# HGRN outputs moved among the value products, HGRN states among the raw products, and the compression done batch by batch

## The reference, cut to what matters

```python
# HGRN2, per head: outputs from products inside a chunk and from the state, and the new state
o     = einsum(A, v) + einsum(q * exp(b), S)
S_new = exp(b_last) * S + einsum(k * exp(b_last - b), v)
o_h   = rms_norm(o, hgrn_norm) * silu(gate)
# NSA compression: 32 raw rows (16 new ones per step) to one key and one value
hid = sum(einsum(chunks[r : r + n] + pe[r], w1[r]) for r in range(2))
out = einsum(silu(hid), w2)                 # kc = rms_norm(out for keys), vc = out for values
```

## Time and profile before

| | us |
|---|---|
| median of 3 runs | 1907.07 (1905.36 to 1914.19) |
| the profiled execution: its time | 1915.5 |
| its span, first to last instruction | 1913.5 |
| TensorE busy | 1779.4 (93%) |
| VectorE busy | 1060.0 (55%) |
| ScalarE busy | 545.4 (29%) |
| GpSimd busy | 143.2 (7%) |
| mean granted TensorE clock | 0.952 of 2.4 GHz |

### The profile page before, as it was taken

The page is one execution under the profiler, slowest core; times in us unless marked ns, Lnnn a source line. Parts: engine busy times, 40 slices in busy tenths (PEclk is TensorE's granted clock), DMA queues, the critical chain, the costliest instruction groups (busy, mean ns, idle before and its releaser), DMA issues.

```text
span 1913.5 us, 28184 instructions
## 1 busy us (share of the span) xinstructions
PE 1779.4 (93%) x11320; PEld 1518.9 (79%) x11320; DVE 1060.0 (55%) x1513; ACT 545.4 (29%) x781; POOL 143.2 (7%) x135
## 2 busy tenths in 40 slices
PE   6999999999769898999999999999999876999998
PEld 6999976776548574468999987999987544999996
DVE  6776623536531664425776636776623734777642
ACT  5443210102101361313343224333211221433321
POOL 1000020000001121101000011110010000000010
PEclk9999998999869898989999999999999788999999
DMA  4445454212234400624677424677433624343432
GB/s 176 153 153 194 143 168 140 82 49 88 103 120 133 149 1 30 216 90 185 234 262 262 154 88 175 237 264 271 151 135 110 261 103 162 130 142 145 175 111 72
DMA packets 50798, 287.80 MB, mean 150 GB/s; under 512 B 8004, under 2 KB 21344, under 8 KB 26624
## 3 DMA queue, kind: packets, MB, share of 16 engines
q1 hardware_dynamic: 41840, 233.90, 33.9%
q0 software_dynamic: 4272, 46.53, 6.7%
q10 hardware_dynamic: 4608, 6.29, 1.0%
HBM read 280.51 MB, written 41.62 MB: 168 GB/s over the span
## 4 chain that ended last, share of the span: by engine, by line
PE 82%; DVE 9%; ACT 3%; DMA 3%; issue 2%; SPq 1%; POOLq 0%; POOL 0%; DVEq 0%; ACTq 0%
PE ps L687 15%; PE ps L689 15%; PE ps L688 15%; PE ps L699 6%; PE ps L1338 6%; PE ps L1387 4%; PE ps L2155 2%; DVE w_lo L678 2%; PE ps L1568 2%; ACT w_hi L672 2%; PE ps L1271 2%; DVE mem L666 1%; PE ps L1696 1%; PE ps L1543 1%; PE ps L885 1%
## 5 line engine op out<-in xcount | busy, mean ns | idle before, releaser
L687 PE MATMUL ps<-x_hi,w_hi 128*128 128x320 f32 x1408 | 439.1, 312 | 29.1 <-DVE w_lo L678 22.3
L688 PE MATMUL ps<-x_lo,w_hi 128*128 128x320 f32 x1408 | 437.4, 311 | 0.0
L689 PE MATMUL ps<-x_hi,w_lo 128*128 128x320 f32 x1408 | 437.2, 311 | 0.0
L678 DVE TENSOR_TENSOR w_lo<-live,w_hi 128x2048 fp32r<-128x2048 f32 (+1 forms) x120 | 300.7, 2506 | 180.7 <-ACT w_hi L672 180.7
L672 ACT ACTIVATE w_hi<-mem 128x2048 fp32r<-128x2048 f32 (+1 forms) x120 | 250.3, 2086 | 259.1 <-DVE mem L666 259.1
L687 PEld LDWEIGHTS ps<-x_hi,w_hi 128*128 128x128 f32 x1408 | 266.2, 189 | 34.4 <-DVE w_lo L678 25.5
L688 PEld LDWEIGHTS ps<-x_lo,w_hi 128*128 128x128 f32 x1408 | 266.4, 189 | 0.0
L689 PEld LDWEIGHTS ps<-x_hi,w_lo 128*128 128x128 f32 x1408 | 266.3, 189 | 0.0
L687 PE MATMUL ps<-act_hi,w_hi 128*128 128x320 f32 x704 | 219.0, 311 | 6.3 <-DVE w_lo L678 6.3
L689 PE MATMUL ps<-act_hi,w_lo 128*128 128x320 f32 x704 | 218.3, 310 | 0.0
L688 PE MATMUL ps<-act_lo,w_hi 128*128 128x320 f32 x704 | 218.2, 310 | 0.0
(11 more groups left out here) (388 smaller groups left out, 2021.8 us busy)
## 6 DMA issues: line engine op xcount, KB each, us to landing
live<-in_w_fi SPq DMA_DIRECT2D x88, 1024.0 KB, 4.8
live<-in_w_fo SPq DMA_DIRECT2D x32, 1408.0 KB, 6.1
mem<-in_dil SPq DMA_DIRECT2D x16, 1152.0 KB, 11.0
out_old_dil<-in_old_dil POOLq DMA_DIRECT2D x8, 2032.0 KB, 9.1
live<-in_w_even SPq DMA_DIRECT2D x12, 1024.0 KB, 4.8
mem<-in_slc SPq DMA_DIRECT2D x48, 192.0 KB, 2.7
live<-in_w_gate SPq DMA_DIRECT2D x8, 1024.0 KB, 4.8
out_old_dil<-in_old_dil POOLq DMA_DIRECT2D x8, 1008.0 KB, 7.5
```

Of the source, the lines that this page charges most:

```text
L678: nc.vector.tensor_tensor(w_lo[:, slot, 0:w], ring[:, slot, 0:w], w_hi[:, slot, 0:w].bitcast(F32), ALU.subtract).then_inc(w_split.sem, 1)
L687: nc.tensor.matmul(out, wh, hi, start=first_k, stop=False)
L688: nc.tensor.matmul(out, wh, lo, start=False, stop=False)
L689: return nc.tensor.matmul(out, wl, hi, start=False, stop=last_k)
```

## The change

Ten parts, as the diff has them.

- **Outputs among value products.** `pe_hgrn_output(c)` is called inside `pe_values`: pairs 0 and 1 after the second and third token tile of chunk 2, pairs 2 and 3 after the second and third of chunk 3. They use banks 6 and 7 in turn, so pair c (2, 3) waits for `hn_done` 9 + c, the multiply of pair c − 2.
- **Their norms are norms 10 to 13** of the same sequence, with banks 4 and 5 and the same tiles and semaphores. Statistics 10 and 11 follow the first and second tile of chunk 3, 12 and 13 the transposes.
- **VectorE.** `dve_hgrn_gate(0)` stands after norm 9, ahead of the last chunk's evacuation; gate 1 after it; then the copies of the transposed keys, gates 2 and 3, and the states.
- **ScalarE.** Page issues of batch 0 (`act_raw(0)`) stand between the root of norm 11 and the square of norm 13.
- **States.** Transposes go to banks 0 to 3, the prompt's states to bank 6, and sample states 2 to 7 stand after each of the six groups of raw batch 0. Raw batch 1 waits for the last of them added.
- **Constants.** `w1c`, `w2c`, `pe_in` lie over the HGRN queries and forget gates, the others over tiles that are dead when the decays are done; SyncE loads them ahead of the stores, on `hg_kd`.
- **Pages.** Batch 1 into `raw[1]` waits for the fourth output only.
- **Prompt's rows first.** They are the 16 extra columns of batch 0, and ScalarE copies them.
- **Per batch.** SiLU, keys, values, squares, root, reciprocal and multiply are done for each batch; on TensorE the keys and values of batch j − 1 follow the fourth group of batch j, its squares the sixth. Those of batch 3 stand in the prompt attention, which begins at the sums of batch 3. Of the fillers, 5 + 6 go and 3 come.
- **Sample attention** waits for all four batches' keys (SyncE's cache loads and TensorE's compressed scores).

```diff
-            pe.wait_ge(hrt_ready.sem, 10)
-            pe.wait_ge(evac.sem, first["even_o", 0])
-            pe_hgrn_outputs(pe)
+            pe_hgrn_turned(pe)
+            pe_head_norm(pe, "even", range(12, 14))
             pe_compress(pe)
...
                     pe_head_norm(pe, which, norms[tt:tt + 1])
+                    if which == "even":
+                        if (j, tt) == (2, 1):
+                            pe_hgrn_output(pe, 0)
+                        elif (j, tt) == (2, 2):
+                            pe_hgrn_output(pe, 1)
+                        elif (j, tt) == (3, 0):
+                            pe_head_norm(pe, which, range(10, 11))
+                        elif (j, tt) == (3, 1):
+                            pe_head_norm(pe, which, range(11, 12))
+                            pe_hgrn_output(pe, 2)
+                        elif (j, tt) == (3, 2):
+                            pe_hgrn_output(pe, 3)
...
+            square(0)
+            for n in range(14):
+                if n == 12:
+                    act_raw(act, 0)
+                if n + 1 < 14:
+                    square(n + 1)
+                act.wait_ge(hms_ready.sem, n + 1)
+                if n >= 2:
+                    act.wait_ge(hn_done.sem, n - 1)
+                nc.scalar.activation(rt2[:, n % 2, :], ps[:, 4 + n % 2, 0:TOK], ACT.Sqrt, bias=eps[:])\
+                    .then_inc(hrt_ready.sem, 1)
...
                     stream("even_v", 0)
+                    sp_compress(sp)
                     sp_save_even(sp)
-                    sp_compress(sp)
...
         def sp_compress(sp):
+            sp.wait_ge(hg_kd.sem, 1)
...
             elif j == 1:
-                cm_loaded.wait(pool, NCM)
+                pool.wait_ge(hg_o.sem, 4)
...
+            pe_hgrn_prompt_states(pe)
+            for hh in range(2):
+                pe_hgrn_sample_state(pe, hh)
             for j in range(NB // 2):
...
-                if j >= 2:
+                if j == 0:
+                    pe.wait_ge(cm_in.sem, 1)
+                elif j == 1:
+                    pe.wait_ge(hg_stc.sem, 5)
+                else:
                     pe.wait_ge(cm_sum.sem, j - 1)
...
+                    if g == 5:
+                        last.then_inc(cm_out.sem, 1)
+                    if j == 0:
+                        pe_hgrn_sample_state(pe, 2 + g)
+                    elif g == 3:
+                        pe_compress_keys_values(pe, j - 1)
+                    elif g == 5:
+                        pe_compress_squares(pe, j - 1)
...
+            for j in range(NB // 2):                    # ScalarE
+                if j + 2 < NB // 2:
+                    act_raw(act, j + 2)
+                act.wait_ge(cm_sum.sem, j + 1)
...
+            for j in range(NB // 2):                    # VectorE
+                dve_compress_sums(dve, j, chain)
+                if j + 1 < NB // 2:
+                    dve_compress_values(dve, j, chain)
+                    dve_compress_keys(dve, j, chain)
...
         def pe_prompt(pe):
-            cm_done.wait(pe)
+            pe.wait_ge(cm_done.sem, 1)
+            pe.wait_ge(cm_sum.sem, NB // 2)
...
             scores(0)
             scores(1)
+            pe_compress_keys_values(pe, NB // 2 - 1)
...
             pe_unread(7, 2)
+            pe_compress_squares(pe, NB // 2 - 1)
...
+                elif t == 0:
+                    pe_unread(7, 3)
+                    pe.wait_ge(cm_vc.sem, NB // 2)
+                    pe.wait_ge(cm_rt.sem, NB // 2)
...
+                if t == 2:
+                    dve_compress_keys(dve, NB // 2 - 1, chain)
```

More of the change, by code:

```diff
@@ L353, in build @@
         pst = sb([P, 3, 12])
+        assert place[0] <= shared + T_Q * TOK
         place[0] = shared + WIN + L_W
@@ new lines, in pe_hgrn_output @@
+        def pe_hgrn_output(pe, c):
+            if c == 0:
+                hg_kd.wait(pe)
+                pe.wait_ge(evac.sem, first["even_v", 0] + 2)
+            if c >= 2:
+                pe.wait_ge(hn_done.sem, 9 + c)
+            for g in range(2):
+                r, hh = slice(64 * g, 64 * g + 64), 2 * c + g
+                v = slice(C_HI + HD * hh, C_HI + HD * hh + HD)
+                o = ps[r, 6 + c % 2, :]
+                nc.tensor.matmul(o[:, 0:TP], vtok[:, 0, v], at[:, hh, 0:TP], start=True, stop=False,
+                                 skip_group_check=True)
+                nc.tensor.matmul(o[:, P:TP], vtok[:, 1, v], at[:, hh, TP:TP + P], start=False, stop=False,
+                                 skip_group_check=True)
+                nc.tensor.matmul(o[:, TP:TOK], vtok[0:64, 2, v], at[0:64, hh, 384:448], start=False, stop=False,
+                                 skip_group_check=True)
+                for b in range(NB):
+                    last = nc.tensor.matmul(o[:, TP + TS * b:TP + TS * b + TS], s0[:, c, b, :],
+                                            qe[:, g, c, TS * b:TS * b + TS], start=False, stop=(b == NB - 1),
+                                            skip_group_check=True)
+            last.then_inc(hg_o.sem, 1)
@@ L1595, in act_compress, with pe_compress_squares @@
-        def act_compress(act):
+        def pe_compress_squares(pe, j):
+            pe.wait_ge(cm_sq.sem, j + 1)
+            if j:
+                pe.wait_ge(cm_rt.sem, j)
+            w = NC_COLS if j == 0 else P
+            nc.tensor.matmul(ps[:, 6, 0:2 * w], ones_h[:], ksq[:, :, 0:w], start=True, stop=True).then_inc(cm_ms.sem, 1)
+        def act_compress(act):
+            for j in range(6):
+                for s2 in range(2):
+                    r = 64 * (j % 2)
+                    src = proj[r:r + 64, T_CMP + j // 2, 0:TP].rearrange("p (m c s t) -> p m s c t", m=2, s=8, t=2)
+                    dst = raw[0][64 * s2:64 * s2 + 64, 2 * PAGES:, 64 * j:64 * j + 64]
+                    last = nc.scalar.activation(dst.rearrange("p m (s c) -> p m s c", s=8), src[:, :, :, :, s2], ACT.Copy)
+            last.then_inc(cm_in.sem, 1)
+            act_raw(act, 1)
@@ new lines, in dve_compress_sums @@
+        def dve_compress_sums(dve, j, chain):
+            n = NC_COLS if j == 0 else 2 * PAST // 16
+            v = ps[:, 2 * (j % 2):2 * (j % 2) + 2, 0:3 * NC_COLS].rearrange("p a (g n) -> p a g n", g=3)
+            dve.wait_ge(cm_out.sem, j + 1)
+            if j:
+                dve.wait_ge(cm_sum.sem, j)
+            chain(nc.vector.tensor_copy(hsum[:, :, :, 0:n - 1], v[64:P, :, :, 1:n]))
+            chain.settle()
+            parts = [(0, NCMP_S, P * j), (64, NCMP_S, P * j + 64)] + [(P, NCMP_P, 512)] * (j == 0)
+            for k, (c, m, to) in enumerate(parts):
+                last = nc.vector.tensor_tensor(hid[:, :, :, to:to + m], v[0:64, :, :, c:c + m], hsum[:, :, :, c:c + m], ALU.add)
+                if k + 1 < len(parts):
+                    chain(last)
+            last.then_inc(cm_sum.sem, 1)
```

308 lines of the change are left out of this document (144 added, 164 removed).

## The result

| | before | changed |
|---|---|---|
| median, us | 1914.37 (20 runs, 1904.49 to 1937.53) | 1904.71 (20 runs, 1890.44 to 1919.07) |
| ratio to before | | 0.9947, 95% interval 0.9927 to 0.9966 |
| profiled execution: time, span | 1915.5, 1913.5 | 1896.5, 1894.5 |
| mean granted clock | 0.952 | 0.959 |

The page's first row for the changed kernel, busy time of each engine, says as little as the mean clock does: TensorE 94% where it was 93%.

A forecast was written before the change was run, and what follows sets the result against it. TensorE, busy 93% of the span, was taken as the bound, leaving gaps and low clock to win: 25.5 + 9.9 − 6.5 − 1 = 27.9 us, from 1907.07 to 1879 us; range 1868 to 1889, with rivals 1 and 2 1865 to 1895.

The forecast's parts named there:

- Up to the first raw product: Stage ending at the first raw product: start at 534 and not 559.5, a gain of 25.5 us.
- 9.9 us: Gain forecast from first raw product to first prompt scores: 69.2 us instead of 79.1.
- ScalarE's page issue for batch 2 ... lies ahead of that SiLU and ends at 557.5, hidden: Before batch 0's SiLU: 7.65 us of page issue costs nothing; TensorE waits 1.5 us before batch 0's keys.
- six sample states of 0.54 each: In raw batch 0: state products added to 12.9 us of raw products, making 16.1 us.
- The wait before keys 1: TensorE's wait for SiLU before the keys and values of batch 1, forecast at 2.9 us.
- 6.5 us lost: From first scores to first transposes: batch 3's keys, squares and fillers at low clock, 14.9 us against 8.4 before.
- 1 us lost: Prompt attention loop: 2 us of VectorE work on batch 3's keys costs 1 us (0 to 2).
- Rival 1: Before raw batch 0: POOL's page issues wait for VectorE, 8 us later, 1887 us; chance 5%.
- Rival 2: Raw batches: serial per-batch chains make waits some 7 us each, 16 us more lost, 1895 us; chance 12%.
- Rival 3: Low clock persists through raw batches, perhaps into the prompt loop: 40 us slower than before, 1947 us; chance 4%.
- Rival 4: Outputs only change place, gaps reappear whole behind gates 2 and 3, nothing won: 1907 us; chance 3%.
- my own signs: Wrong if first transposes come under 18 us earlier, clock low in raw batches 1–3, or later stages change over 2 us.

The follow-up runs named there:

- e5: Changed kernel, ScalarE issuing batch 2's pages before waiting for the position bias, and hidden rows over dead tiles, not waiting for the sample states' store; 1898.29 us, ratio 0.9901.
- e12: Changed kernel with the edits of e5 and e9, odd pages issued by SyncE, sample state products in pairs, fillers before outputs 2 and 3, first keys, scores; 1868.85 us, 0.9772.
- e8: Changed kernel plus products nobody reads before the keys of batches 0 and 1 (8 and 3) and before the first scores (5); 1889.77 us, ratio 0.9871.
- e9: Changed kernel, but VectorE computes batch 3's keys ahead of turn 0 of the prompt attention instead of in turn 2; 1892.36 us, ratio 0.9889.
- e6: Changed kernel, all batches' keys, values, squares, roots, reciprocals after the last raw product, pages of batches 2 and 3 issued together ahead of the SiLUs; 1894.96 us, 0.9895.
- e1: Changed kernel, but ScalarE issues the pages of batch 2 before it waits for the position bias; 1901.16 us, ratio 0.9941.
- e2: Changed kernel, hidden rows over dead tiles so their sums skip waiting for the sample states' store, prompt's state stored early; 1906.65 us, ratio 0.9969.
- e11: e6 plus the edit of e9 and fillers before outputs 2 and 3 (2 and 4) and the first scores (5); 1881.20 us, ratio 0.9827.

## Why the prediction was wrong, step by step

*Up to the first raw product: right in its waits, in part by luck in its sum.* From output 0 on, 58.7 us forecast, 58.2 measured; waits of 1.5 and 4.2 forecast, 1.52 and 4.00 measured. The place of the clock was off. It had fallen by 498, behind the 1.52 us wait already, came back near 504 and fell again behind the second wait; output 2 was slower than I had it, and the constants were faster, 3.7 us for the 7.0 of the earlier trace rows. A wait of 1.82 us for VectorE's spread values, which I had ready by then, was missing. That these cancel to 0.5 us is luck.

*"9.9 us" from there to the first scores: wrong, it was a loss of 4.3* (83.6 us against 79.3 before and 69.2 forecast). The terms:
- "ScalarE's page issue for batch 2 ... lies ahead of that SiLU and ends at 557.5, hidden" is the step that failed. I had started it when the pages' slots were free. It starts behind the bias, the bias behind L1022 (3.3 us, in neither row nor working), and with the read of the first page's number it takes 9.1 us and not 7.65 (the issues alone 7.82). It ended at 565.5, and the wait was 8.18 us, not 1.5. The store, which I had taken for the limit at 4.25 us, took 6.8, and its chain ended 3 us ahead of the page issue's. e5, which edits both chains, and e12 show it.
- "six sample states of 0.54 each": 1.07 each, as long as two in the earlier trace rows. Batch 0 took 20.4 us and not 16.1, with 1.4 of it the first group at the low clock. This and the wait make up the 10.4 us by which R to the first keys was too short (36.8 for 26.4).

```profile
535.14 1.07 PE L1344 MATMUL ps<-mem 64*64 64x512 f32 x2
536.14 2.23 PE L1615 MATMUL ps<-live,mem 128*128 128x144 f32 x16
```

- No low clock behind the waits was priced here, and this is the second step that failed. The two groups behind keys 0 took 5.51 us and those behind keys 1 6.27, where 3.8 was in the sum. From the first keys to the scores that is 46.7 us for 42.8. e8, with the clock held, has 40.3 there, and 10.2 for 14.1 behind the scores. Its R to first scores is 76.8 us: the clock is 6.8 of the 14.4 us by which that stretch was too short.
- The wait before keys 1 was 3.71 for 2.9, the scores' 4.99 for 4.7: sound.

*"6.5 us lost" behind the first scores:* 14.9 forecast, 14.1 measured. Right.

*"1 us lost" in the loop:* 7.9. The delay of 1.84 us is what I had bounded by 2; that TensorE then runs at half speed for some 13 us was not in the bound, although the trace of before shows the same thing behind the statistics gaps. e9 takes all of it back.

*The rivals.* Rival 1 did not happen: in 516.3 to 528.4, with VectorE busy 10.3 of 12.1 us, POOL's page issues stand 1.14 us apart, as in the earlier trace rows. From 508.5 to 516.4 they stand 1.5 to 2.5 us apart, with VectorE busy only 2.9 of 9.0 us; ScalarE's eight issues run beside them (506.8 to 517.8), and in the kernel before the same pattern stands beside ScalarE's issues at 491.8.

```profile
516.30:528.40 12.10, 11.64 (x64) 10.36 (x62) 10.26 (x15) 6.37 (x15) 5.93 (x11) 0.67 0.85 283
```

```profile
518.68 0.54 POOL L1561 DMA_DIRECT2D live<-in_cmp  x1 [0.61 <-issue]
...
524.40 0.54 POOL L1561 DMA_DIRECT2D mem<-in_cmp  x1 [0.60 <-issue]
```

Rival 2 is what happened, in its first wait rather than in all three: 8.2 and 3.7 us, and none over 1 us before the keys of batch 2, for its 7 each. Its sum left out the clock as the forecast's did. Rival 3 held in part: its condition (low at the second raw batch) was not met throughout, but the clock fell anew behind each wait. I had treated the low level as one event with one recovery. Rival 4, that the gaps reappear whole behind gates 2 and 3, did not happen: those waits were as forecast. Two thirds of the expected gain went all the same, behind other releasers. By my own signs the forecast was wrong at once: transposes 17.8 us earlier, and low clocks in raw batches 1 to 3.

## What to carry to other kernels

Where a change cuts one long wait of the matrix engine into several short ones, price each new wait with its own duration and, as a bound, with the half-speed stretch that can follow it (in e6 none behind 2.97 us among raw products, over 20 us behind 1.85 us in the loop), and look for idle gaps on the helper engine (here: ahead of turn 0) before placing even 2 us of work into a loop whose engine has none. Before costing an issue block as hidden, walk its engine's queue back: every wait that stands ahead of it, what that wait's producer has queued, and whether the block needs it at all. When one wait has two candidate causes, edit both together once, since each alone may show nothing (e1: 1.4 us, e2: 1.1, both: 4.9).

## What the runs showed of the hardware

- TensorE's clock left 2.4 GHz behind idle times of 1.52 and 1.84 us, and then stayed at 1.2 GHz under steady work for some 7 us (after the first), 13 (after the stall in the changed kernel's loop) or over 20 (after the same stall in e2 and e6, whose T to G is 88.3). The length of the wait alone does not decide it: 2.97 us (e6) and 2.31 us (e11) between raw products, and the 1.51 us before output 2 in e5, left the clock at 1.00. What decides whether it falls and for how long these runs do not show.
- Two 64-row, 64-column products into different halves of the array overlap: 1.08 us for two and 1.07 us for one alone. Six lone ones cost 3 us.
- The same DMA work took different times with different neighbours: the eight page issues of batch 2 on ScalarE 7.63 us (e2), 7.82 (changed), 9.91 (e5) and 10.21 (e1), longest where they lie over the store; the 1 MB store 4.25 us before the change, with no page loads beside it, and 4.8 (e2), 5.7 (e5), 6.8 (changed) and 8.4 (e1) beside them.
- A switch of ScalarE's function cost 1.28 us in every row, with the next instruction 0.01 to 0.02 us behind it where that waited for nothing else (565.51, next 566.80). The Trainium skill (ScalarE: Activation LUTs, "What ACT_TABLE_LOAD costs") gives 1.28 us for the load, which agrees, and a drain of 1.38 us more with each switch, which no row here shows as a gap before or behind the load.
- The Trainium skill (SBUF — State Buffer, "A bandwidth-pool intuition that's wrong") has a DMA issued from GpSimd starved of descriptors while VectorE copies between SBUF tiles. Most of VectorE's time in the window above was not such copies, so it only weighs against a general form of that rule; what the runs show is that 10.3 of 12.1 us of VectorE work changed nothing in the 1.14 us pitch.
